# The Conformer's 31 taps: four taps and 32 channels on the contraction, from shifted copies

## The reference

```python
def conformer_conv(h, w_in, b_in, dw, dw_b, ln_g, ln_b, w_out, b_out):
    u = h @ w_in + b_in
    u = u[..., :D_MODEL] * jax.nn.sigmoid(u[..., D_MODEL:])
    u = depthwise_conv(u, dw, dw_b)
    u = jax.nn.silu(layer_norm(u, ln_g, ln_b))
    return u @ w_out + b_out
```

## Time and profile before

| | us |
|---|---|
| median of 3 timed runs | 2193.52 (2193.38 to 2196.08) |
| profiled execution, its own time | 2196.92 |
| its span | 2195.2 |
| TensorE matmul busy | 2015.6 (92%) |
| VectorE busy | 1279.9 (58%) |
| ScalarE busy | 994.9 (45%) |
| GpSimd busy | 747.3 (34%) |

### The profile page before, as it was taken

One profiled execution on the slowest core, in us unless ns is written; L12 is line 12 of the kernel. 1 busy time (PEld: TensorE's weight loads), 2 busy tenths in 40 slices (PEclk: granted clock), 3 DMA queues, 4 the chain that ended last, 5 costly groups with the idle time before them and its releaser, 6 DMA issues.

```text
span 2195.2 us, 30850 instructions
## 1 busy us (share of the span) xinstructions
PE 2015.6 (92%) x11973; PEld 1813.9 (83%) x11973; DVE 1279.9 (58%) x1911; ACT 994.9 (45%) x1767; POOL 747.3 (34%) x568
## 2 busy tenths in 40 slices
PE   3789999999978878899999998799999979899998
PEld 1579998799977866799987997599998766699986
DVE  0567761566328866677724795377751686577732
ACT  1344442554336633544424686354442535544432
POOL 0133324333327655333343840233334320333242
PEclk6889999999989989999999999899999988999999
DMA  9953336433310134643365500643446322243332
GB/s 370 374 212 125 125 120 244 162 121 124 125 62 26 40 120 157 237 144 122 119 225 178 196 19 1 278 173 125 125 163 220 145 109 81 86 144 125 124 126 77
DMA packets 77073, 320.98 MB, mean 146 GB/s; under 512 B 8672, under 2 KB 14208, under 8 KB 63104
## 3 DMA queue, kind: packets, MB, share of 16 engines
q1 hardware_dynamic: 76048, 318.18, 41.3%
q10 hardware_dynamic: 880, 0.82, 0.1%
HBM read 314.96 MB, written 4.01 MB: 145 GB/s over the span
## 4 chain that ended last, share of the span: by engine, by line
PE 77%; DVE 9%; ACT 5%; DMA 4%; issue 2%; POOL 1%; SPq 1%; DVEq 0%; ACTq 0%
PE pair L1675 16%; PE pair L1677 16%; PE pair L1676 16%; PE pair L1709 6%; PE pair L1710 6%; PE pair L1711 6%; DMA mod_more<-in_w_mod 2%; PE pair L1798 2%; DVE x L1246 2%; PE pair L1896 1%; PE pair L1895 1%; PE pair L1894 1%; PE pair L1831 1%; ACT junk L848 1%; DMA raw<-in_ssd_out 1%
## 5 line engine op out<-in xcount | busy, mean ns | idle before, releaser
L675 POOL TENSOR_TENSOR w_lo<-raw,w_hi 128x512 fp32r<-128x512 f32 (+1 forms) x375 | 578.2, 1544 | 1205.5 <-ACT w_hi L820 1205.5
L1675 PE MATMUL pair<-h_hi,w_hi 128*128 128x386 f32 (+1 forms) x2008 | 687.6, 342 | 19.1 <-POOL h_lo L682 19.1
L1677 PE MATMUL pair<-h_hi,w_lo 128*128 128x386 f32 (+1 forms) x2008 | 683.4, 340 | 0.0
L1676 PE MATMUL pair<-h_lo,w_hi 128*128 128x386 f32 (+1 forms) x2008 | 682.8, 340 | 0.0
L1179 DVE TENSOR_TENSOR w_lo<-raw,w_hi 128x512 fp32r<-128x512 f32 x351 | 426.6, 1217 | 335.9 <-ACT w_hi L820 335.9
L820 ACT ACTIVATE w_hi<-raw 128x1024 fp32r<-128x1024 f32 x375 | 393.0, 1050 | 294.2 <-PE pair L1711 213.0
L1675 PEld LDWEIGHTS pair<-h_hi,w_hi 128*128 128x128 f32 (+1 forms) x2008 | 380.6, 190 | 23.6 <-POOL h_lo L682 22.3
L1676 PEld LDWEIGHTS pair<-h_lo,w_hi 128*128 128x128 f32 (+1 forms) x2008 | 381.5, 190 | 0.9
L1677 PEld LDWEIGHTS pair<-h_hi,w_lo 128*128 128x128 f32 (+1 forms) x2008 | 380.8, 190 | 0.3
L1303 DVE SCALAR_TENSOR_TENSOR acc<-pair,taps,acc 128x385 f32<-128x385 f32 x176 | 108.9, 619 | 213.1 <-ACT acc L907 213.1
L907 ACT ACTIVATE acc<-pair,taps 128x386 f32<-128x386 f32 x176 | 117.3, 667 | 236.7 <-PE pair L1677 236.7
(11 more groups left out here) (254 smaller groups left out, 2557.1 us busy)
## 6 DMA issues: line engine op xcount, KB each, us to landing
raw<-in_ffn_in SPq DMA_DIRECT2D x176, 512.0 KB, 3.5
raw<-in_ffn_out SPq DMA_DIRECT2D x88, 512.0 KB, 3.6
mod_raw<-in_w_mod SPq DMA_DIRECT2D x32, 1024.0 KB, 7.7
mod_base<-in_w_mod SPq DMA_DIRECT2D x31, 1024.0 KB, 7.3
mod_more<-in_w_mod SPq DMA_DIRECT2D x20, 1024.0 KB, 13.8
raw<-in_ssd_conv SPq DMA_DIRECT2D x32, 512.0 KB, 3.5
gb<-rows_dram SPq DMA_DIRECT2D x8, 1024.0 KB, 5.4
raw<-in_ssd_z SPq DMA_DIRECT2D x16, 512.0 KB, 3.5
```

The costliest lines, as they stand in the source:

```text
L675: pool.tensor_tensor(w_lo[:, m % SLOTS, 0:w], raw[:, m % SLOTS, 0:w], w_hi[:, m % SLOTS, 0:w].bitcast(F32), ALU.subtract).then_inc(w_low_p ...
L1675: ten.matmul(to, wh, h_hi[:, k, cols], start=k == 0, stop=False, skip_group_check=True)
L1676: ten.matmul(to, wh, h_lo[:, k, cols], start=False, stop=False, skip_group_check=True)
L1677: ins = ten.matmul(to, wl, h_hi[:, k, cols], start=False, stop=k == KD - 1, skip_group_check=True)
```

## The change

TensorE takes five tiles (3 to 7) and VectorE three (0 to 2). For a tile of TensorE the 128 channels are four quarters q of 32. The contraction of one matmul is 4 taps x 32 channels: partition 32 r + c holds channel c of the quarter shifted by r columns. SP makes these with 16 copies per tile (4 shifts x 4 quarters, each 32 partitions x 428 columns of fp32, 55 KB) from glu to shifted, which has three slots. The 31 taps are eight groups t of four (one tap is zero). The stationary matrix tap_diag is 128x32 (four 32x32 diagonals one above the other), the moving one is shifted from column 4t on, 400 columns, fp32 without a split. The four quarters write the four quarters of one bank's partitions. VectorE makes tap_diag from ident4 at the start of the stage. The products of tiles 3, 4 and 5 stand behind chunks 11, 13 and 15 in TensorE's list, those of tiles 6 and 7 after. The mean takes TensorE's tiles first and VectorE's last. linear_half and gate_half get a third slot.

```diff
-CONV_PE = 4
-CONV_DVE = KD - CONV_PE
-CONV_GROUPS = [(0, 1), (2, 3)]
-HALF_SLOTS = 2
+CONV_DVE = 3
+CONV_PE = KD - CONV_DVE
+QUARTER = 4
+LANES = P // QUARTER
+TAP_GROUPS = -(-TAPS31 // QUARTER)
+SHIFTED = CONVOLVED + QUARTER * (TAP_GROUPS - 1)
+GLU_W = SHIFTED + QUARTER
+SHIFT_SLOTS = 3
+CONV_BEHIND = 5
+HALF_SLOTS = 3
 CONVOLVED_AT = [at - REACH for at in CGAP_AT]
-C_BIN = KD * TAPS31
+C_TAPS = CONV_DVE * TAPS31
+C_BIN = C_TAPS + CONV_PE * QUARTER * TAP_GROUPS
...
-            glu_hi = sb("glu_hi", [P, CONV_PE, CGAP], F32R, part)
-            glu_lo = sb("glu_lo", [P, CONV_PE, CGAP], F32R, part)
-            tap_hi = sb("tap_hi", [P, CONV_PE * TAPS31], F32R, part)
-            tap_lo = sb("tap_lo", [P, CONV_PE * TAPS31], F32, part)
-            diagonal = sb("diagonal", [P, TAPS31, 2, P], F32R, part)
-            glu = sb("glu", [P, KD, CGAP], F32, part)
+            ident4 = sb("ident4", [P, LANES], F32, part)
+            shifted = sb("shifted", [P, SHIFT_SLOTS, QUARTER, SHIFTED], F32, part)
+            tap_diag = sb("tap_diag", [P, CONV_PE, QUARTER, TAP_GROUPS, LANES], F32, part)
+            glu = sb("glu", [P, KD, GLU_W], F32, part)
...
+        def conv_behind(j):
+
+            k = (j - CONV_BEHIND) // 2 - CONV_DVE
+            return k if j % 2 and 0 <= k < CONV_PE else None
...
-                    load_to(s.n0 + s.chunks)
+                    for k in range(CONV_PE):
+                        m = CONV_DVE + k
+                        load_to(s.n0 + 2 * m + 6)
+                        sp.wait_ge(glu_ready, 1 + 2 * m + 2)
+                        if k >= SHIFT_SLOTS:
+                            sp.wait_ge(pe_tap, k - SHIFT_SLOTS + 1)
+                        for r in range(QUARTER):
+                            for q in range(QUARTER):
+                                sp.dma_start(shifted[r * LANES:(r + 1) * LANES, k % SHIFT_SLOTS, q, :],
+                                             glu[q * LANES:(q + 1) * LANES, m, r:r + SHIFTED]
+                                             ).then_inc(shift_loaded[k % SHIFT_SLOTS], 16)
...
-                    if m > CONV_DVE:
-                        glu_low(m - CONV_DVE - 1)
                     pool.wait_ge(evac, EVAC_CONF + 2 * m + 2)
...
-                    if m == 0:
-                        pool.wait_ge(tap_hi_ready, 1)
-                        pool.tensor_tensor(tap_lo[:, :], conf_tab[:, CONV_DVE * TAPS31:KD * TAPS31],
-                                           tap_hi[:, :].bitcast(F32), ALU.subtract).then_inc(tap_lo_ready, 1)
-                glu_low(CONV_PE - 1)
-
-            def glu_low(k):
-                pool.wait_ge(glu_hi_ready, k + 1)
-                pool.tensor_tensor(glu_lo[:, k, :], glu[:, CONV_DVE + k, :], glu_hi[:, k, :].bitcast(F32),
-                                   ALU.subtract).then_inc(glu_lo_ready, 1)
...
-                act.activation(tap_hi[:, :], conf_tab[:, CONV_DVE * TAPS31:KD * TAPS31], ACT.Copy).then_inc(tap_hi_ready, 1)
-
...
+                def conv_evac(k):
+                    m = CONV_DVE + k
+                    act.wait_ge(pe_tap, k + 1)
+                    act.activation(convolved[:, m, :], bank(4 + k % 2)[:, 0:CONVOLVED], ACT.Identity,
+                                   bias=conf_tab[:, C_DWB + m:C_DWB + m + 1]).then_inc(pe_conv, 1)
+
+                done_conv = 0
                 for m in range(2 * KD):
+                    if m and conv_behind(m - 1) is not None:
+                        conv_evac(done_conv)
+                        done_conv += 1
                     act.wait_ge(w_used, s.n0 + m + 1)
                     gated, tile = m % 2, m // 2
                     if tile >= HALF_SLOTS:
@@ -1021,23 +1020,8 @@
                     if m == 3:
                         copy_row(6)
                     round_to(s.n0 + m + 5)
-                    if m >= 4:
-                        act.wait_ge(tap_lo_ready, 1)
-                        for _ in range(3):
-                            if made < TAPS31:
-                                diagonals(0, made)
-                                made += 1
-                    if m >= 2 * CONV_DVE + 2 and m % 2 == 0:
-                        glu_high(tile - CONV_DVE - 1)
-                glu_high(CONV_PE - 1)
...
+                for k in range(done_conv, CONV_PE):
+                    conv_evac(k)
...
-                for group in CONV_GROUPS:
...
+                ch.did(vec.tensor_tensor(ident4[:, :], ident[:, 0:LANES], ident[:, LANES:2 * LANES], ALU.add))
+                for q in range(2, QUARTER):
+                    ch.wait()
+                    ch.did(vec.tensor_tensor(ident4[:, :], ident4[:, :], ident[:, q * LANES:(q + 1) * LANES], ALU.add))
+                ch.wait()
+                for k in range(CONV_PE):
+                    at = C_TAPS + k * QUARTER * TAP_GROUPS
+                    width = QUARTER * TAP_GROUPS
+                    vec.tensor_tensor(tap_diag[:, k, :, :, :].rearrange("p q t c -> p (q t) c"),
+                                      ident4[:, :].unsqueeze(1).broadcast_to([P, width, LANES]),
+                                      conf_tab[:, at:at + width].unsqueeze(2).broadcast_to([P, width, LANES]),
+                                      ALU.mult).then_inc(diag_ready, 1)
+                low_to(lin["conf_in"].n0 + 2 * KD + SLOTS)
+                for m in range(CONV_DVE):
+                    vec.wait_ge(glu_ready, 1 + 2 * m + 2)
+                    vec.tensor_scalar(convolved[:, m, :], glu[:, m, 0:CONVOLVED], conf_tab[:, m * TAPS31:m * TAPS31 + 1],
+                                      conf_tab[:, C_DWB + m:C_DWB + m + 1], ALU.mult, ALU.add).then_inc(conf_tap, 1)
+                for k in range(1, TAPS31):
+                    for m in range(CONV_DVE):
+                        vec.wait_ge(conf_tap, CONV_DVE * (k - 1) + m + 1)
+                        vec.scalar_tensor_tensor(
+                            out=convolved[:, m, :], in0=glu[:, m, k:k + CONVOLVED],
+                            scalar=conf_tab[:, m * TAPS31 + k:m * TAPS31 + k + 1],
+                            in1=convolved[:, m, :], op0=ALU.mult, op1=ALU.add).then_inc(conf_tap, 1)
...
+                def conv(k):
+                    if k >= 2:
+                        ten.wait_ge(pe_conv, k - 1)
+                    ten.wait_ge(diag_ready, k + 1)
+                    ten.wait_ge(shift_loaded[k % SHIFT_SLOTS], 16 * QUARTER * QUARTER * (k // SHIFT_SLOTS + 1))
+                    b = bank(4 + k % 2)
+                    for t in range(TAP_GROUPS):
+                        for q in range(QUARTER):
+                            ins = ten.matmul(b[q * LANES:(q + 1) * LANES, 0:CONVOLVED], tap_diag[:, k, q, t, :],
+                                             shifted[:, k % SHIFT_SLOTS, q, QUARTER * t:QUARTER * t + CONVOLVED],
+                                             start=t == 0, stop=t == TAP_GROUPS - 1, skip_group_check=True)
+                    ins.then_inc(pe_tap, 1)
+
+                def mean_part(m, first, last):
+                    if m >= CONV_DVE:
+                        ten.wait_ge(pe_conv, m - CONV_DVE + 1)
+                    else:
+                        ten.wait_ge(conf_tap, CONV_DVE * (TAPS31 - 1) + m + 1)
+                    return ten.matmul(bank(6)[:, 0:CONVOLVED], ones[:, :], convolved[:, m, :], start=first, stop=last)
+
+                convolved_tiles = 0
                 for j in range(2 * KD):
                     if j >= 4:
                         ten.wait_ge(evac, EVAC_CONF + j - 3)
                     in_tile(s, j, 3)
-                for t in range(CONV_PE):
-                    ten.wait_ge(glu_lo_ready, t + 1)
-                    if t >= 2:
-                        ten.wait_ge(pe_conv, t - 1)
-                    b = bank(4 + t % 2)[:, 0:CONVOLVED]
-                    for k in range(TAPS31):
-                        ten.wait_ge(diag_ready, t * TAPS31 + k + 1)
-                        first, last = k == 0, k == TAPS31 - 1
...
-                places = [*range(2), *range(CONV_DVE, KD), *range(2, CONV_DVE)]
-                for i, m in enumerate(places):
-                    if m >= CONV_DVE:
-                        ten.wait_ge(pe_conv, m - CONV_DVE + 1)
-                    else:
-                        ten.wait_ge(conf_tap, TAPS31 * max(g[-1] + 1 for g in CONV_GROUPS if m in g))
-                    ins = ten.matmul(bank(6)[:, 0:CONVOLVED], ones[:, :], convolved[:, m, :], start=i == 0, stop=i == KD - 1)
+                    if conv_behind(j) is not None:
+                        conv(conv_behind(j))
+                        convolved_tiles += 1
+                for k in range(convolved_tiles, CONV_PE):
+                    conv(k)
+                for m in range(CONV_DVE, KD):
+                    mean_part(m, m == CONV_DVE, False)
+                for m in range(CONV_DVE):
+                    ins = mean_part(m, False, m == CONV_DVE - 1)
                 ins.then_inc(ln_sum, 1)
...
+    dw = np.zeros((QUARTER * TAP_GROUPS, D), np.float32)
```

(27 more changed lines are left out.)

## The result

The changed kernel takes 2237.49 us (median of four, 2222.32 to 2237.66) against 2193.45 (four, 2190.28 to 2196.08): a ratio of 1.0184, 95% interval 1.014 to 1.0229 (taken over all runs, the one of 2222.32 too; the medians alone give 1.020). It is slower, well clear of no change; whether by 2% or more these runs leave open. I had forecast 2177 and faster. The profiled execution's span is 2235.9 us.

The account below looks back on a forecast made before the run. TensorE alone was taken to bound the stage; in the new kernel SP's copy loop sets the pace: glu at 1247.2, loops 65.2, copies 6.4, landing 2.3, clock 2.2, last tile 5.7 give 1329.0, 16.6 us gained: 2177 us, range 2160 to 2198.

Parts of the forecast that it names:

- one tap passes for each GpSimd instruction, and the rest run in its free time: VectorE's taps beside GpSimd: 21 taps in GpSimd's 39 us, the other 70 in 37.1 us.
- the issue time of a copy: SP's queue: 0.33 us plus a 0.07 gap, 0.40 for each of 80 copies; bounds 0.33 and 0.60.
- The forecast's sum: Conformer convolution: glu of tile 3 at 1247.2, loops, copies, landing, clock loss and last tile end at 1329.0, before 1345.6.
- Four loops: From glu of tile 3 to glu of tile 7: 4 x 16.3 = 65.2 us, ending at 1312.4.
- TensorE's form: The new fp32 products, four column parts side by side: 0.71 us a group, 5.7 a tile, 28.5 in all.
- the second estimate: TensorE's new products by the Trainium skill's page on column parts: 0.87 us a group, 7.0 us a tile.
- that rival, 2236: TensorE's four parts don't run side by side: 22.1 us a tile, 110 us in all; chance 0.04.
- Clock behind the pause: TensorE's last tile after standing for 10 us: 2.2 us added for a reduced clock.
- SP's loop: Glu to next glu through 16 copy issues, load, rounding, w_lo and glu: 16 d + 9.9, 16.3 us a tile.
- "dear issue" rival: SP's queue: issues of small copies cost more, 8 us per 0.1 us of d; slower from 0.61 us; chance 0.13.
- VectorE's last tap at 1314: End of VectorE's three tiles: 1313.7, ahead of TensorE's last product, so not the last path.
- 1:1 behind the mean: The mean and all that follows stay as they were, so the 16.6 us gained ahead carry through.

Follow-up runs that it names:

- experiment four: Changed kernel with SP's weight loads two chunks further ahead and each VectorE tap waiting for the one two places before: 2190.58 us, ratio 0.9987.
- experiment five: Changed kernel with each VectorE multiply-add waiting for the one right before it, not three back: 2192.67 us, ratio 0.9993.
- experiment seven: Changed kernel with weight loads two chunks further ahead and VectorE's running sums in PSUM banks 6, 7 and 4: 2162.25 us, ratio 0.9843.

## Why the prediction was wrong

The step that failed is VectorE's: "one tap passes for each GpSimd instruction, and the rest run in its free time". I had it from the kernel before, where it gave 1330.3 against 1330.8. There GpSimd was busy for 7.4 to 10 of each 10 us, mostly with its next instruction ready when one ended. Its longest pause in the train was 2.63 us, ahead of the w_lo at the place of the later hold, and that one got in:

```profile
1242.57 2.80 POOL L675 TENSOR_TENSOR w_lo<-raw,w_hi 128x1024 fp32r<-128x1024 f32 x1 [2.63 <-ACT w_hi L820]
```

In the new kernel the same w_lo comes after a pause of 3.93 us and is held for 47.62. The rule described turns between two engines that are both at work, and I took it for an arrival from a pause too; experiment four shows both outcomes of such an arrival in one train.

The second step that failed is the issue time of a copy, 0.63 us where the sum has 0.40. By itself it takes the whole gain away, as the list below shows.

The forecast's sum against the trace: end of the last product 1385.5, forecast 1329.0, 56.5 more. Glu of tile 3 at 1291.7 and not 1247.2: 44.5. Four loops of 18.6, not 16.3: 9.2. From glu of tile 7 to the start of its product 11.5, not 8.7: 2.8. The last product 7.97 against 7.9.

By its other steps:
- *TensorE's form.* Right: 64 records in 5.58 us at full clock, 0.70 a group (0.71 said, and not the 0.87 of the second estimate). Four parts do run side by side. The time of that rival, 2236, was met by chance, by another mechanism.
- *Clock behind the pause.* Right: 7.97 us for the last tile, 2.4 above the 5.58 of full clock (2.2 said).
- *SP's loop.* Right in mechanism and mis-sized in one term: an issue is 0.59 us and 0.63 with its gap, where I took 0.40. The 16 issues and the gap to the load take 10.2 us of the loop's 18.6, not 6.4; the other terms take 8.4, not 9.9. The closest row was the store from on-chip memory (0.604), not the short ones that I went by. The 2.1 us of the first issues came in none of the 80 copies (longest 0.622). At 0.63 the forecast's sum is 2195 (its own "dear issue" rival, which it gave 0.13), and experiment five, which is that kernel without the hold, has 2192.67. So even without the hold the change as made gains nothing.
- *VectorE's last tap at 1314.* 1287.7 with the hold, 1317.1 with a pause at each tap, and 1282.5 in PSUM. Two slips in the working: 1237.25 + 39 + 37.1 is 1313.4, and a free tap takes 0.546 us, not 0.53, as the 38 taps counted in 20 us include some that lie only partly in the window.
- *1:1 behind the mean.* Right: the mean's end moved by 40.0 us (1351.1 to 1391.1), the span by 40.7.

What stays open: what decides whether an instruction that arrives gets in. In the trains without pauses, arrivals after at most 2.63 us of pause all got in, those after 3.39 to 3.63 got in twice and were held once, and the three after 3.78 to 5.25 were held. That is too few to call the length of the pause the cause. Nor is it traced why some runs of one kernel lie 13 to 17 us apart (2222.32 beside 2237.5; 2210 beside 2193); that holds of other lengths cause it is argued only.

## What to carry to other kernels

A rule of turns read from a trace holds for the load that it was read under. When a change gives one of two engines on a shared port longer pauses, it must be read anew, or the sharing taken away: running sums in PSUM made both engines free. The price was three banks, which left one for TensorE's tiles (0.7 us of waiting for an evacuation in experiment seven) and made the mean wait for the last tap. Before a set of small DMAs goes into a queue of weight loads, follow who waits for the load behind it, and let that load go first; with the sums in PSUM this was worth 29.5 us (2191.75 to 2162.25).

## What the runs showed of the hardware

- A GpSimd instruction with SBUF operands was held for 38 to 48 us by a train of VectorE instructions with two SBUF inputs, 0.546 us apart, in four traces. With one instruction in three started 0.12 us later (rounds of 1.76 us), the trace has no hold and the four timed runs (2163.51 to 2166.84) show no sign of one; nor do the 14 runs with the second input in PSUM (2158.37 to 2166.13 and 2191.03 to 2195.42).
- A VectorE tensor_scalar of 128x400 from SBUF to SBUF took 2.55 us beside a w_lo that had started before it, and 0.70 with its output in PSUM (experiment seven).
- A copy from SBUF to SBUF of 32 rows costs its queue 0.59 us, whether the rows have 1712 or 2048 bytes, against 0.328 for a weight load of 128 rows of 4 KB; it lands after 1.9 us.
